# Normalized tiles scaled by two engines, Fourier sums taken token tile by token tile, and the last product by column halves

## The chip, the cores and the metric

The kernel runs on one NeuronCore of one Trainium2 chip. The metric is the device time of one execution in microseconds; a number for a kernel is the median of several runs. One execution was also taken by the hardware profiler, and all times of single instructions come from that one.

## The reference, cut to what matters

The program is two transformer blocks over 256 tokens of width 1024, in float32. The first block has two mixers (a gated linear recurrence and a spatial gate), a gated feed-forward part and a gated embedding; the second has a Fourier mixer, a retention mixer and two feed-forward parts. What the change touches:

```
h = rmsnorm(x, g) * (1 + scale) + shift        # at each boundary; the first block has no scale and shift
f = fftn(h.reshape(B, S, 4, 256), axes=(1, 3), norm="ortho").real     # Fourier mixer
x = x + gate * (f.reshape(B, S, D) @ w_fourier_out)
x = x + gate * swiglu(modulate(rmsnorm(x)))    # feed-forward, the last product is "down2"
return modulate(rmsnorm(x, final_norm_g), shift_final, scale_final)
```

The real part of the Fourier transform is a sum of products with cosine and sine tables: first over the 256 features of a group, then over the 256 tokens.

## The kernel before

**Weights.** All weights come through one stream of 238 chunks of 1 MB (128 x 2048 float32), issued by SP in a fixed order into three `raw` buffers; a buffer is free when `raw_done` says that its chunk was split. A chunk is split in two parts for TensorE: ScalarE copies it rounded (`w_hi`, L743), VectorE subtracts (`w_lo`, L1097). `tick(w)` does this for chunk `w + 4`, on ScalarE and on VectorE, and it stands at fixed places in each engine's program; four chunks of `w_hi` and `w_lo` are kept. The order of work on each engine is written out by hand, and an engine never takes a later instruction first.

**Products.** Each product is three matmuls (low by high, high by high, high by low). There are two token tiles of 128. `outer` (L477) takes the two tiles of a product into one of two PSUM `pair` buffers each, with the last four chunks first for tile 0 and then for tile 1. `wide_part` (L416) takes one chunk for one token tile: twelve matmuls of 512 columns, over half of the 1024 features.

**Boundaries.** At a boundary (`norm0` to `norm6`) the residual of a tile is updated (L1187, L1189, or L1177, L1180 in the first block), ScalarE squares it (L765), VectorE makes the mean (L1124), GpSimd the power (L355), VectorE scales it to `xn` (L1134). TensorE turns `xn` to features by partitions: eight transposes (L495), in two jobs of four, each in one of three `tp` banks. In `scaled` (L1145) VectorE then multiplies each of the eight 128 x 128 quarters with a column constant, and adds one where there is a shift, and leaves them in `hb` (or in `outb` at the end). For each half ScalarE rounds `hb` to `ht_hi` (L761) and VectorE subtracts to `ht_lo` (L1157), as `norm_his` and `norm_jobs`. `turned_head` starts the next product and waits for both halves of a tile before its first matmul. A quarter is one instruction; a half has four.

**Fourier mixer.** For tile 0, TensorE multiplies the four feature groups with the tables (L654, job `dft1`), then makes the gate rows (L517, job `rows0`), then turns tile 1, then the features of tile 1 (`dft1b`). The results are split to `tt_hi` and `tt_lo`. Only then come the token sums (L668, job `dft2`), for both tiles together in `tp` banks, which are split to `ht_hi` and `ht_lo` for the product `fo`. The modulation of tile 0 (`norm2`) is turned behind chunk 1 of the second tile of product `pleg`.

**The end.** After the last product `down2`, the second tile's residual, square, mean, power, `xn`, turn and eight quarters follow one another, each over the full width; four output transfers (L341) go out by SP.

Semaphores touched: `norm_read` and `fin_read` count halves read by VectorE; `lo_done` counts all splits; `w_used` the chunks used; `half_ready` tile 0 of a product.

## Time and profile before

| | us |
|---|---|
| median of 3 runs | 1191.15 (1190.08 to 1191.34) |
| profiled execution, own time | 1189.39 |
| span of that execution | 1187.2 |
| TensorE busy | 1146.8 |
| VectorE busy | 851.0 |
| ScalarE busy | 521.0 |
| a weight chunk, issue to landing | 4.9 |

The span runs from the first to the last instruction; the execution's own time is 2.2 us longer. A row of a timeline says when an instruction started, how long it took, its engine, line, what it wrote and read, how many were merged in it, and in brackets how long the engine had been idle and what ended that.

### The profile page before, as it was taken

The page shows a single profiled execution, that of the slowest core. Times are in us where ns is not written, and L with a number is a line of the kernel's source. Part 1 is how long each engine was busy: PE and PEld are TensorE (multiplying, and loading weights), DVE is VectorE, ACT ScalarE, POOL GpSimd, SP SyncE. Part 2 cuts the span into 40 slices and gives each one's busy share as a digit, 9 for nine tenths or more (in the row PEclk, how much of TensorE's full clock was granted, in tenths as well). Part 3 has the DMA queues.
Part 4 walks back from the last instruction along what each step waited for, and adds up shares of the span by engine and source line. Part 5 has one row for each costly group of instructions (what it writes and reads, how often), then busy time and mean ns, then how long its engine had stood idle before and what let it go on. Part 6 is the DMA issues. An engine that isn't in the chain of part 4 may idle for free.

```text
span 1187.2 us, 13991 instructions
## 1 busy us (share of the span) xinstructions
PE 1146.8 (97%) x5824; PEld 965.3 (81%) x5824; DVE 851.0 (72%) x1009; ACT 521.0 (44%) x463; POOL 27.4 (2%) x51
## 2 busy tenths in 40 slices
PE   6999999999899999998999999999999999999996
PEld 5898998888688888877778888879976887888885
DVE  5789988986667677575657767478955867767755
ACT  5556555634444344444343434334423433434430
POOL 1000000000000000000000000000001000000000
PEclk8999999999999999999999999999999999999998
DMA  8754563547357768532357777448753563786761
GB/s 310 280 213 163 187 231 130 176 167 269 142 205 258 301 265 316 204 141 72 138 181 272 262 305 290 191 177 320 278 202 122 212 249 142 255 311 259 287 234 36
DMA packets 38638, 259.81 MB, mean 219 GB/s; under 512 B 4144, under 2 KB 6448, under 8 KB 7856
## 3 DMA queue, kind: packets, MB, share of 16 engines
q1 hardware_dynamic: 36960, 251.84, 57.0%
q0 software_dynamic: 1616, 7.08, 1.6%
q8 instruction: 46, 0.75, 0.2%
q14 instruction: 16, 0.13, 0.0%
HBM read 257.86 MB, written 1.05 MB: 218 GB/s over the span
## 4 chain that ended last, share of the span: by engine, by line
PE 85%; DVE 9%; issue 3%; ACT 2%; DMA 1%; POOL 0%; SPq 0%; DVEq 0%; POOLq 0%; ACTq 0%
PE pair L416 41%; PE pair L477 24%; PE pair L442 10%; DVE w_lo L1097 4%; PE tp L495 2%; PE tp L554 2%; DVE hb L1145 2%; PE tp L716 1%; PE tp L668 1%; DMA raw<-stream 1%; ACT w_hi L743 1%; PE tp L581 1%; ACT ht_hi L761 1%; PE tp L694 1%; DVE ht_lo L1157 1%
## 5 line engine op out<-in xcount | busy, mean ns | idle before, releaser
L1097 DVE TENSOR_TENSOR w_lo<-raw,w_hi 128x2048 fp32r<-128x2048 f32 x182 | 412.8, 2288 | 92.8 <-ACT w_hi L743 92.6
L743 ACT ACTIVATE w_hi<-raw 128x2048 fp32r<-128x2048 f32 x182 | 347.6, 1916 | 223.9 <-DMA raw<-stream 133.3
L416 PE MATMUL pair<-w_hi,ht_lo 128*128 128x512 f32 x816 | 327.9, 402 | 20.8 <-DVE w_lo L1097 12.2
L416 PE MATMUL pair<-w_lo,ht_hi 128*128 128x512 f32 x816 | 319.8, 392 | 0.0
L416 PE MATMUL pair<-w_hi,ht_hi 128*128 128x512 f32 x816 | 319.7, 392 | 0.0
L416 PEld LDWEIGHTS pair<-w_hi,ht_lo 128*128 128x128 f32 x816 | 154.3, 189 | 57.6 <-issue 14.7
L416 PEld LDWEIGHTS pair<-w_lo,ht_hi 128*128 128x128 f32 x816 | 154.2, 189 | 33.1
L416 PEld LDWEIGHTS pair<-w_hi,ht_hi 128*128 128x128 f32 x816 | 154.5, 189 | 31.3 <-issue 1.2
L477 PE MATMUL pair<-w_hi,gt_lo 128*128 128x512 f32 x360 | 142.3, 395 | 0.2 <-DVE gt_lo L1163 0.2
L477 PE MATMUL pair<-w_lo,gt_hi 128*128 128x512 f32 x360 | 140.3, 390 | 0.0
L477 PE MATMUL pair<-w_hi,gt_hi 128*128 128x512 f32 x360 | 140.1, 389 | 0.0
L1106 DVE SCALAR_TENSOR_TENSOR raw<-raw,crow 128x1024 f32<-128x1024 f32 x112 | 132.4, 1220 | 1.3 <-DMA raw<-stream 1.3
L1218 DVE TENSOR_TENSOR prod<-prod,pair 128x512 f32<-128x512 f32 x33 | 22.7, 689 | 111.2 <-ACT prod L842 111.2
L842 ACT ACTIVATE prod<-pair 128x512 f32<-128x512 f32 x33 | 19.7, 598 | 179.1 <-PE pair L416 179.1
L442 PE MATMUL pair<-ht_hi,w_lo 128*128 128x256 f32 x320 | 91.0, 284 | 0.0
L442 PE MATMUL pair<-ht_lo,w_hi 128*128 128x256 f32 x320 | 90.6, 283 | 0.0
L442 PE MATMUL pair<-ht_hi,w_hi 128*128 128x256 f32 x320 | 90.6, 283 | 0.0
L477 PEld LDWEIGHTS pair<-w_hi,gt_lo 128*128 128x128 f32 x360 | 67.6, 188 | 14.6 <-DVE gt_lo L1163 0.7
L477 PEld LDWEIGHTS pair<-w_lo,gt_hi 128*128 128x128 f32 x360 | 67.6, 188 | 14.3
L477 PEld LDWEIGHTS pair<-w_hi,gt_hi 128*128 128x128 f32 x360 | 67.7, 188 | 14.1 <-issue 0.5
L442 PEld LDWEIGHTS pair<-ht_hi,w_hi 128*128 128x128 f32 x320 | 61.4, 192 | 0.1
L442 PEld LDWEIGHTS pair<-ht_hi,w_lo 128*128 128x128 f32 x320 | 61.4, 192 | 0.1
(201 smaller groups left out, 1101.8 us busy)
## 6 DMA issues: line engine op xcount, KB each, us to landing
raw<-stream SPq DMA_DIRECT2D x238, 1024.0 KB, 4.9
xres<-x SPq DMA_DIRECT2D x2, 512.0 KB, 6.8
prow<-rows POOLq DMA_DIRECT2D x1, 1024.0 KB, 9.7
xres<-x POOLq DMA_DIRECT2D x2, 512.0 KB, 4.9
dt<-decay POOLq DMA_DIRECT2D x1, 1024.0 KB, 7.1
outT<-outb SPq DMA_DIRECT2D x4, 256.0 KB, 2.2
csr<-dft POOLq DMA_DIRECT2D x1, 768.0 KB, 4.4
crow<-rows POOLq DMA_DIRECT2D x1, 512.0 KB, 6.4
```

What stands on the lines that cost most here:

```text
L416: mm = pe.matmul(pair[use % 2][:, t, :], a[:, 4 * c + k, t * P:(t + 1) * P], b[:, w % WS, k * 512:(k + 1) * 512], start=(c == 0 and k == 0 ...
L442: mm = pe.matmul(pair[use % 2][:, c, m * S:(m + 1) * S], a[:, k, m * P:(m + 1) * P], b[:, k, :], start=(k == 0 and n == 0), stop=(k == KT ...
L477: mm = pe.matmul(pair[(use + t) % 2][:, half, :], src(a, k0 + 2 * c + k, t), wsp[b][:, (w + c) % WS, k * D + half * 512:k * D + half * 512 ...
L495: mm = pe.transpose(tp[k % BANKS][:, n * P:(n + 1) * P], a, idn[:])
L554: mm = pe.matmul(tp[k % BANKS][:, hd * P:(hd + 1) * P], sk[:, hd, s * P:(s + 1) * P], sq[:, hd, s * P:(s + 1) * P], start=True, stop=True)
L581: mm = pe.matmul(tp[k % BANKS][:, hd * P:(hd + 1) * P], at[:, s, hd, t * P:(t + 1) * P], vv[:, s, (HH * half + hd) * P:(HH * half + hd + 1 ...
L743: sc.activation(w_hi[:, w % WS, :], raw[:, n % RAW, :], ACT.Copy).then_inc(hi_done, 1)
L842: sc.activation(prod[:, j % 2, :, :], pair[(use + j) % 2][:, :, 0:256], ACT.Silu).then_inc(silu_done, 1)
L1097: v.tensor_tensor(w_lo[:, w % WS, :], raw[:, n % RAW, :], whi32[:, w % WS, :], ALU.subtract).then_inc(raw_done, 1)
L1106: ins = v.scalar_tensor_tensor(out=src, in0=src, scalar=1.0, in1=crow[:], op0=ALU.mult, op1=ALU.mult, accum_out=mod[:, 2 * a + half:2 * a ...
L1145: ins = v.tensor_scalar(dst(k, half)[:, m * P:(m + 1) * P], tp[k % BANKS][:, m * P:(m + 1) * P], scale[:, f:f + 1], None if shift is None ...
L1218: v.tensor_tensor(prod[:, j % 2, :, :], prod[:, j % 2, :, :], pair[(use + j) % 2][:, :, 256:512], ALU.mult).then_inc(evac[(use + j) % 2], 1)
```

## The change

- Each tile's second half of quarters goes to ScalarE: `norm_scaled` scales (and shifts) four quarters with `Identity` activations, between the two `ht_hi` of the tile. VectorE's `scaled` keeps the first half. Two semaphores `norm_act` and `fin_act` count ScalarE's halves.
- `turned_head` waits for each half of a tile's features by itself, in front of the chunk that needs it.
- `norm_jobs` can put a `tick` between the two `ht_lo` (`between`), at norm1, norm3, norm4 and norm5. At norm1 other ticks move as well, on both engines.
- Fourier mixer: the turn of `norm2` tile 0 stands half a chunk later; token sums are taken for one token tile at a time, and accumulate in the two `pair` buffers that the product `fo` uses; the gate rows come after them; the ticks move.
- Boundary constants (`columns`) are made ahead of the residual.
- `down2` takes tile 1's last four chunks by column halves (`outer_by_halves`); the last residual, square and `xn` go by halves; eight matmuls on `ones` stand before the last turn.

The diff, cut to its core:

```diff
@@ PSUM jobs
-             ("rows0", 2, "row_copied"), ("norm2b", 2, "norm"), ("dft1b", 4, "split"), ("dft2", 4, "split"),
+             ("norm2b", 2, "norm"), ("rows0", 2, "row_copied"), ("dft1b", 4, "split"),
@@ turned_head
-                wait_split(split, 2)
                 for c in range(4):
                     wait_chunk(w + c)
+                    if c < 2:
+                        wait_split(split, c + 1)
...
-                wait_split(split, 4)
                 for c in range(4):
+                    if c < 2:
+                        wait_split(split, 3 + c)
@@ new: outer_by_halves, behind the last t == 0 chunk
+                for c in range(n - 4, n):
+                    mm = part(c, 1, 0)
+                mm.then_inc(last_half, 1)
+                for c in range(n - 4, n):
+                    part(c, 1, 1).then_inc(w_used, 1)
+                    if c == n - 3:
+                        tail()
@@ pleg and Fourier, TensorE
-                         (1, 1): turn_tile("norm2", xn, 0, xn_done, 5)})
+                  between={(2, 1): turn_tile("norm2", xn, 0, xn_done, 5)},
...
+            features("dft1", 0)
+            wait_evac(pe, USE["pleg"])
+            wait_evac(pe, USE["pleg"] + 1)
+            tokens("dft1", 0, (0, 1))
+            turn_tile("norm2", xn, 1, xn_done, 6)()
+            tokens("dft1", 0, (2, 3))
+            gate_rows("rows0", 1)
+            wait_split("norm2b", 2)
+            features("dft1b", 1)
+            tokens("dft1b", 1, range(4))
             outer(W0["fo"], 4, USE["fo"], tiles(ht),
-                  before={(c, 0): lambda c=c: wait_split("dft2", c + 1) for c in range(4)},
+                  before={(c, 0): lambda c=c: pe.wait_ge(mix_lo, max(c + 1, 2)) for c in range(4)},
@@ last turn, TensorE
-            turn_tile("norm6", xn, 1, xn_done, 14)()
+            for _ in range(8):
+                pe.matmul(warm[:, 384:512], ones[:], ones[:], start=True, stop=True)
+            for half in range(2):
+                pe.wait_ge(xn_done if half else xn_half, {0: 1, 1: 14}[half])
+                turn(tile_job("norm6", 1) + half, [xn[:, 1, (4 * half + k) * P:(4 * half + k + 1) * P] for k in range(4)])
@@ ScalarE
+            def norm_scaled(name, t, scale, shift, dst):
+                k = tile_job(name, t) + 1
+                act.wait_ge(tp_done, k + 1)
+                if k in SPLIT:
+                    at_least(act, lo_done, SPLIT[k] - 1)
+                for m in range(4):
+                    f = 4 + m
+                    ins = sc.activation(dst[:, m * P:(m + 1) * P], tp[k % BANKS][:, m * P:(m + 1) * P], ACT.Identity,
+                                        scale=scale[:, f:f + 1], bias=0.0 if shift is None else shift[:, f:f + 1])
+                ins.then_inc(sem(RELEASE[k][0]), 1)
+            def norm_his(name, t, scale, shift=None):
+                norm_hi(name, t, 0)
+                norm_scaled(name, t, scale, shift, hb[:, (tile_job(name, t) + 1) % 2, :])
+                norm_hi(name, t, 1)
@@ ScalarE, Fourier, after norm_his("norm2", t)
+            gate_rows("rows0", grow[0])
+            dft_his("dft1b", 1, (0, 1, 2))
+            tick(w - 2)
+            dft_his("dft1b", 1, (3,))
...
+            mix_his((0, 1))
+            tick(w - 1)
+            mix_his((2, 3))
+            tick(w)
@@ VectorE
+            def norm_jobs(name, t, scale, shift=None, between=None):
+                k = tile_job(name, t)
+                scaled(name, t, scale, shift, hb[:, k % 2, :])
+                dve.wait_ge(norm_read, RELEASE[k][1])
+                norm_lo(name, t, 0)
+                if between is not None:
+                    tick(between)
+                norm_lo(name, t, 1)
@@ VectorE, norm1
-                norm(RQ["mix"] + 2 * t + 1, t, w + 2 if t else None)
+                norm(RQ["mix"] + 2 * t + 1, t, w + 2 if t else w)
                 if t:
                     tick(w + 3)
-                norm_jobs("norm1", t, colv("ffn_pre", 0, 8))
-                if t == 0:
-                    tick(w)
-                    tick(w + 1)
+                norm_jobs("norm1", t, colv("ffn_pre", 0, 8), between=None if t else w + 1)
@@ VectorE, Fourier
                 norm_jobs("norm2", t, moda[:, 0, :], mod[:, 0:8])
-                if t == 0:
-                    tick(w - 3)
+            tick(w - 3)
+            dft_los("dft1b", 1, (0, 1, 2))
+            tick(w - 2)
+            dft_los("dft1b", 1, (3,))
@@ VectorE, boundary
+                if columns is not None:
+                    columns()
                 gated_post(0, use, w, halves, row, rows)
                 norm(q, 0)
-                if columns is not None:
-                    columns()
-                norm_jobs(name, 0, scale, shift)
-                tick(w - 3)
+                norm_jobs(name, 0, scale, shift, between=w - 3)
                 tick(w - 2)
@@ VectorE, last tile, for half in range(2)
+                dve.wait_ge(w_used, W0["down2"] + GROUPS) if half else dve.wait_ge(last_half, 1)
+                part = slice(half * 512, (half + 1) * 512)
+                link(v.tensor_tensor(xn[:, 1, part], pair[use % 2][:, half, :], grow[1][:, part], ALU.mult))
+                v.tensor_tensor(xres[:, 1, part], xres[:, 1, part], xn[:, 1, part], ALU.add).then_inc(x_ready, 1)
+                dve.wait_ge(ss_done, SS[q] + half)
```

## Rows read from the trace of the kernel before

**Rows 1.** The head of the page: span; busy time and instructions of each engine.

```profile
span 1187.2 us, 13991 instructions
PE 1146.8 (97%) x5824; PEld 965.3 (81%) x5824; DVE 851.0 (72%) x1009; ACT 521.0 (44%) x463; POOL 27.4 (2%) x51
```

**Rows 2.** Waits of TensorE: total us, times, longest.

```profile
PE pair L416 <- DVE w_lo L1097: 12.2, 5, 7.2
```

**Rows 3.** The chain that ended last: start, duration, instructions merged.

```profile
542.40 5.78 PE tp L654 x24
548.18 11.51 PE tp L668 x96
...
620.61 10.92 PE pair L416 x48
```

**Rows 4.** Timeline of TensorE at norm4.

```profile
775.32 0.47 PE L416 MATMUL pair<-w_hi,ht_lo 128*128 128x512 f32 x1 [0.53 <-issue]
...
782.07 0.50 PE L416 MATMUL pair<-w_hi,ht_lo 128*128 128x512 f32 x1 [1.02 <-DVE w_lo L1097]
...
789.77 0.50 PE L416 MATMUL pair<-w_hi,ht_lo 128*128 128x512 f32 x1 [1.02 <-DVE ht_lo L1157]
```

**Rows 5.** Timeline of VectorE at norm4.

```profile
768.91 2.64 DVE L1145 TENSOR_SCALAR hb<-tp,moda,mod 128x128 f32<-128x128 f32 x8 [0.75 <-PE tp L495]
...
772.93 4.49 DVE L1097 TENSOR_TENSOR w_lo<-raw,w_hi 128x2048 fp32r<-128x2048 f32 x2
777.33 1.22 DVE L1187 TENSOR_TENSOR xn<-pair,grow 128x1024 f32<-128x1024 f32 x1
```

**Rows 6.** Groups of ScalarE by form: busy us, mean ns, idle before.

```profile
L761 ACT ACTIVATE ht_hi<-hb 128x512 fp32r<-128x512 f32 x24 | 15.0, 630 | 35.4 <-DVE hb L1145 35.2
...
L752 ACT ACTIVATE vr<-pair 128x1024 f32<-128x1024 f32 x4 | 4.1, 1020 | 11.1 <-PE pair L416 11.1
...
L752 ACT ACT_TABLE_LOAD x2 | 2.6, 1283 | 0.0
```

**Rows 7.** Timeline of ScalarE and VectorE at the start, norm0 tile 0.

```profile
12.08 1.13 ACT L761 ACTIVATE ht_hi<-hb 128x512 fp32r<-128x512 f32 x2
...
14.00 4.49 DVE L1097 TENSOR_TENSOR w_lo<-raw,w_hi 128x2048 fp32r<-128x2048 f32 x2
```

**Rows 8.** Timeline of VectorE and TensorE at norm1.

```profile
304.46 4.49 DVE L1097 TENSOR_TENSOR w_lo<-raw,w_hi 128x2048 fp32r<-128x2048 f32 x2
...
306.84 0.47 PE L416 MATMUL pair<-w_hi,ht_lo 128*128 128x512 f32 x1 [2.79 <-issue]
...
314.47 0.50 PE L416 MATMUL pair<-w_hi,ht_lo 128*128 128x512 f32 x1 [1.91 <-DVE w_lo L1097]
...
323.23 0.50 PE L416 MATMUL pair<-w_hi,ht_lo 128*128 128x512 f32 x1 [0.53 <-DVE ht_lo L1157]
```

**Rows 9.** Sums over a stretch at norm1, with the granted clock (PEclk).

```profile
315.00:319.00 4.00, 4.00 (x12) 3.06 (x11) 2.95 (x2) 0.20 (x1) 0.11 (x1) 0.57 0.73 262
```

**Rows 10.** Timeline of TensorE from the turn of norm2 to tile 1's features.

```profile
522.07 0.66 PE L495 MATMUL tp<-idn,xn 128*128 128x128 f32 x4 [1.01 <-DVE xn L1134]
...
536.64 1.12 PE L517 MATMUL tp<-dg,ones 128*128 128x512 f32 x2 [1.59 <-DVE tt_lo L1163]
...
542.40 0.50 PE L654 MATMUL tp<-cs_hi,ht_lo 128*128 128x512 f32 x1 [3.76 <-DVE ht_lo L1157]
```

**Rows 11.** Timeline of VectorE and TensorE behind the last product.

```profile
1175.44 1.23 DVE L1187 TENSOR_TENSOR xn<-pair,grow 128x1024 f32<-128x1024 f32 x1 [0.48 <-PE pair L477]
...
1180.76 1.97 PE L495 MATMUL tp<-idn,xn 128*128 128x128 f32 x8 [5.36 <-DVE xn L1134]
...
1181.92 2.64 DVE L1145 TENSOR_SCALAR outb<-tp,moda,mod 128x128 f32<-128x128 f32 x8 [1.21 <-PE tp L495]
```

**Rows 12.** Transfers on the page: KB each, median us from issue to landing.

```profile
raw<-stream SPq DMA_DIRECT2D x238, 1024.0 KB, 4.9
```

More of the change, by code:

```diff
@@ L135, in plan_psum @@
                 splits += 1
-            sem = {"norm": "norm_read", "split": "lo_done"}.get(kind, kind)
+            half = (k - jobs[name]) % 2
+            sem = {"norm": ("norm_read", "norm_act")[half], "fin_read": ("fin_read", "fin_act")[half],
+                   "split": "lo_done"}.get(kind, kind)
             if kind == "split":
@@ L455, in turned_head, with outer @@
                         norm()
-                wait_split(split, 4)
                 for c in range(4):
+                    if c < 2:
+                        wait_split(split, 3 + c)
                     wide_part(w + c, use + c // 2, c % 2, 1)
-            def outer(w, n, use, src, k0=0, before={}, after={}):
+            def outer(w, n, use, src, k0=0, before={}, between={}, after={}):
                 m = max(0, n - 4)
@@ L474, in outer @@
                     for half in range(2):
+                        if half and (c, t) in between:
+                            between[c, t]()
                         for k in range(2):
@@ L642, in _, with features @@
                   before={(0, 0): lambda: wait_split("tx", 2), (0, 1): lambda: wait_split("tx", 4)},
-                  after={(1, 0): turn_tile("tx", xres, 1, x_ready, 4),
-                         (1, 1): turn_tile("norm2", xn, 0, xn_done, 5)})
+                  between={(2, 1): turn_tile("norm2", xn, 0, xn_done, 5)},
+                  after={(1, 0): turn_tile("tx", xres, 1, x_ready, 4)})
             wait_split("norm2", 2)
             pe.wait_ge(cs_done, 1)
-            for t in range(TT):
+            def features(name, t):
                 for gr in range(4):
-                    k = JOB["dft1b" if t else "dft1"] + gr
+                    k = JOB[name] + gr
                     claim(k)
@@ L905, in head_gates, with boundary @@
                 tick(W0[b] + 1)
-            def boundary(w, q, name, n_x):
+            def boundary(w, q, name, n_x, scale, shift):
                 norm_squares(q, 0, n_x)
@@ L912, in boundary @@
                 tick(w - 2)
-                norm_his(name, 0)
+                norm_his(name, 0, scale, shift)
                 tick(w - 1)
@@ L916, in boundary @@
                 tick(w)
-                norm_his(name, 1)
+                norm_his(name, 1, scale, shift)
             def gated_chunks(half, name0, plan):
@@ L1062, in _ @@
                 tick(w)
-            boundary(W0["ro"] + 7, RQ["norm5"], "norm5", 11)
+            boundary(W0["ro"] + 7, RQ["norm5"], "norm5", 11, moda[:, 3, :], mod[:, 72:80])
             ffn("ffn2", "h2")
@@ L1070, in _ @@
                     hidden_his("h2", GROUPS - 1)
-            for t in range(TT):
-                norm_squares(RQ["norm6"] + t, t, 13 + t)
+            norm_squares(RQ["norm6"], 0, 13)
+            norm_scaled("norm6", 0, moda[:, 4, :], mod[:, 96:104], outb[:, 1, :])
+            for half in range(2):
+                act.wait_ge(x_ready, 14 + half)
+                part = slice(half * 512, (half + 1) * 512)
+                sc.activation(xn[:, 1, part], xres[:, 1, part], ACT.Square,
+                              accum_out=st[:, RQ["norm6"] + 1, 0, half:half + 1]).then_inc(ss_done, 1)
+            norm_scaled("norm6", 1, moda[:, 4, :], mod[:, 96:104], outb[:, 3, :])
         @block.vector
@@ L1150, in norm_jobs @@
-            def norm_jobs(name, t, scale, shift=None):
-                scaled(name, t, scale, shift, lambda k, half: hb[:, k % 2, :])
-                for half in range(2):
-                    k = tile_job(name, t) + half
-                    dve.wait_ge(norm_read, RELEASE[k][1])
-                    dve.wait_ge(t_hi, SPLIT[k] + 1)
-                    where = (slice(None), slice(4 * half, 4 * half + 4), slice(t * P, (t + 1) * P))
-                    v.tensor_tensor(ht[1][where], hb[:, k % 2, :].rearrange("p (k s) -> p k s", k=4), ht32[where],
-                                    ALU.subtract).then_inc(lo_done, 1)
+                k = tile_job(name, t)
@@ new lines, in scaled @@
+                dve.wait_ge(tp_done, k + 1)
+                if k in SPLIT:
+                    at_least(dve, lo_done, SPLIT[k] - 1)
+                for f in range(4):
+                    ins = v.tensor_scalar(dst[:, f * P:(f + 1) * P], tp[k % BANKS][:, f * P:(f + 1) * P],
+                                          scale[:, f:f + 1], None if shift is None else shift[:, f:f + 1],
+                                          ALU.mult, *(() if shift is None else (ALU.add,)))
+                ins.then_inc(sem(RELEASE[k][0]), 1)
```

188 lines of the change are left out of this document (114 added, 74 removed).

## The prediction

> **What bounds the kernel now.** I read the page first. TensorE is busy 1146.8 us of a 1187.2 us span, VectorE 851.0 [rows 1], so an edit pays only where it shortens TensorE's queue of work or takes out one of its waits. About 40 us are waits, and the list of waits puts the largest entry, 12.2 us in five places, on VectorE's weight splits `w_lo` [rows 2]. The timeline shows where: none inside the long products, all at the normalization boundaries, at the Fourier stage, at the start and at the end. So I walked these places in the timelines of the three engines.
>
> Two paces carry the rest. Forty-eight matmuls of 512 columns take 10.92 us, 0.227 us each, so one weight chunk for one token tile (12 of them) is 2.73 us [rows 3]. An idle time in a row counts from a modelled end 0.17 us after the next possible start, so a stall is its idle time plus 0.17.
>
> **The boundaries of norm3, norm4 and norm5** look alike; I use norm4. TensorE stalls three times there, idle 0.53, 1.02 and 1.02 us [rows 4], or 0.70, 1.19 and 1.19 by start times. VectorE's order is the cause: eight `hb` quarters (2.64 us), two `ht_lo`, then both `w_lo` (4.49 us) from 772.93, then the second tile's residual at 777.33 [rows 5]. The first stall waits for the first `w_lo`, the second for the third, the last for tile 1's `ht_lo`.
>
> The change gives four quarters to ScalarE, lets the product start after half the features, and puts `tick(w-3)` between the two `ht_lo`. VectorE's four quarters take 1.32, from 768.91 to 770.27. ScalarE's `ht_hi` (0.63 [rows 6]) ends at 770.94, `ht_lo` needs 0.61 net of overlap, and the first `w_lo` ends at 773.87, before TensorE's 774.63. Stall one is gone. The second `ht_lo` and `w_lo` end by 776.6, so the residual starts 0.74 earlier than 777.33. All that follows up to the third `w_lo` is one chain on VectorE and keeps that 0.74: TensorE goes on at 781.33, not 782.07, having waited 1.25. TensorE arrives 0.69 earlier and stall two stays about as long as it was. On tile 1 the first `ht_lo` comes at 787.65; TensorE needs it at 787.84. Stall three (1.19) goes, with a margin of 0.2 only. Its second half has one chunk, 2.73 us, more. Gain 1.93 for a boundary; norm5 gets 0.05 more because its constants move from behind `xn` into an idle wait. Three boundaries: **5.85** (4.5 if the 0.2 is missed by half a microsecond each time, 6).
>
> **ScalarE's four quarters** have no row. The 128x1024 form takes 1.02 and the 128x512 `hb` form 0.63 [rows 6]; two forms of 512 back to back overlap by 0.1 (1.13 for two at the start [rows 7]). Taken down to 128 columns this gives 0.27 for one and 0.81 for four; as slow as four full 512-column ones it is 2.1. What two pointer operands cost on ScalarE no row shows. I take the middle, 1.45. VectorE's constants cost time too (four with two constants 1.32), so I don't go to the low end.
>
> The Trainium skill, page "ScalarE: Activation LUTs", section "What ACT_TABLE_LOAD costs", says that each per-partition pointer operand adds 93 ns, which speaks against moving scale and shift here: by it four take 1.64 us with both and 1.27 with a scale alone, and the sum below would fall by about 0.6 us.
>
> **norm1** has other stalls: TensorE idle 2.79 and 1.91, then 0.53 [rows 8]. `tick(w)` moves ahead of the mean square: that `w_lo` (2.2) fills an idle 1.2 and delays `xn` of tile 0 to 300.82, so the turn waits 0.6 us, a new stall. But the next product's first chunk is then split, and its `ht_lo` is there at 304.0: TensorE starts it at 304.5, not 306.84. VectorE then has one `w_lo` and four quarters fewer before the mean square, which comes at 306.72 rather than 308.86. ScalarE's second square pass needs `hi` of half 1 first and ends at 306.3, in time. The chain behind it keeps the 2.14, so TensorE resumes at 312.33 after a 2.40 stall. With stall three gone (0.69) that is 2.83. In the profile the clock stood at 0.57 of full speed in 315 to 319 us, right behind the idle 1.91 [rows 9]; twelve matmuls took 4.45 instead of 2.9, a loss of 1.5. The new stall is longer but single; whether the clock falls there I can't tell. I count a quarter of it: **3.2** (2.8 to 4.3).
>
> **norm0** loses. VectorE's first `w_lo` waits behind both `ht_lo` (from 14.00 [rows 7]), and the second now waits for ScalarE's `ht_hi` (end 12.71 for the first), four quarters and another `ht_hi`: `w_lo` begins at about 15.4 and TensorE at 17.7 instead of 16.43, 1.27 later. TensorE runs there at half speed until 21.7, so the late start costs between half of this and all; the stall before tile 1 (0.70) goes. Net **-0.4** (-1.2 to +0.2).
>
> **Fourier stage.** Removed: a stall before the turn of tile 0 (idle 1.01), one before the gate rows (1.59) and one before tile 1's features (3.76) [rows 10]. The turn now sits half a chunk later, at 522.26, behind `xn`'s end at 522.02. The last product ends at 527.2 rather than 528.4; tile 0's second `ht_lo` goes over ScalarE (524.96 + 1.45 + 0.63 + 0.69, with handovers 527.7), so 0.55 is waited. Then TensorE has 24 feature matmuls (5.46), half the token sums of tile 0 (2.9), a turn (0.85), the other half (2.9), the gate rows (1.75), features (5.46) and token sums (5.76). A group of 24 took 5.78 and all 96 token matmuls 11.51 [rows 3]; their number is unchanged, only their order, and they accumulate in the two `pair` banks. That adds to 25.1, end 552.85, against 559.53. Covers: the `xn` of tile 1 is ready at 534.65, the turn comes at 536.1. Its second `ht_lo` comes at 541.5, the token sums and gate rows cover it to 541.6. The last `tt_lo` is behind `tick(w-2)` and comes at 551.5, 0.15 late. `tick(w-3)` moves from 527.9 to 541.4, past `dft1`, the norm and their queues: VectorE frees its raw slot at 543.7 only, so SP, which waits for `raw_done` in stream order, issues the next chunk fourteen microseconds later. With 4.9 us to land [rows 12] it is there by 549, split by 558.3 and wanted at 560.8. `gate_rows` on ScalarE goes behind the norm, and features 1 and 2 of tile 1 now claim its banks; the copies end by 542, wanted at 543 and 544.4. The new wait on `mix_lo` needs two `ht_lo` by 552.45, before the sums end. **6.5** (5.3 with 2.1 for the quarters, 7.1 with 0.81).
>
> **The end.** TensorE's order in the last product changes, not its work: columns 0 to 511 of tile 1 are ready at 1169.1, the rest at 1175.44 as before. But VectorE's four quarters of tile 0 stand ahead in its queue until 1173.63. Then half 0: two ops of 0.69 and ScalarE's square reach 1175.7, VectorE waiting for `ss_done` with half 1's product queued behind it; half 1 so starts at 1175.95, and not at 1175.44, and its square is read at 1178.12; before it was 1179.11. `xn` comes in halves of 0.45, so the first turn starts at 1179.47 against 1180.76 [rows 11]. Eight matmuls on ones keep TensorE busy to about 1177. Before, eight transposes took 1.97 there, against 1.09 elsewhere. Warm, ScalarE ends its quarters at 1181.95, cold at 1182.9; before, VectorE ended at 1184.56, and 2.64 us of output DMA follow in both cases. Gain 2.6 or 1.7: **2.2** (1.0 to 2.9).
>
> **Sum.** -0.4 + 3.2 + 6.5 + 5.85 + 2.2 = 17.35 us. The span becomes 1169.85, the profiled execution's own time 1189.39 - 17.35 = 1172.0. The median of the runs shown is 1.76 above that execution, so I forecast 1191.15 - 17.35 = **1173.8 us**. The low and high ends of the terms give 12.4 and 20.5, 1178.8 and 1170.7.
>
> **Rivals.**
> - The sums of the Fourier stage don't cover: lo parts in ScalarE's and VectorE's strict order come late once more, as 3.76 shows they do today. With half of that stage's 6.5 lost: 1177.1. Chance 0.15.
> - The quarters take 2.1: start -0.65, Fourier -1.2, end -0.65, boundaries nothing: 1176.3. Chance 0.12.
> - Slower: ScalarE loads a table around the scaled copies. A load takes 1.28 [rows 6]. Up to 2.2 us for the four, the boundaries hide them; beyond it each microsecond costs about 12 (two tiles at six places). The gain left at 2.2, 14.4 us, is gone at 3.4 us. Two loads around each group make 4.0: 7 us slower, 1198. Against it: `Copy` and `Square` run among Silu, Gelu, Exp and Sigmoid everywhere here, and ScalarE has eleven loads in 463 instructions [rows 1, 6], none ahead of a `Copy`; a scaled copy is of that kind. Chance 0.05, of which 0.04 slower and 0.01 about even.
> - The clock stays up at norm1 and the plain runs lose more to it than the profiled one: 1171.3. Chance 0.06.
>
> For the table load, the same page of the Trainium skill, "Table sets: the hidden batching unit", says that identity and copy are in every set, so no load would come; that agrees with the rows of `Copy`.
>
> The forecast itself keeps 0.62, with 1172 to 1176 of its own. The range that leaves out two in ten at most is **1170.5 to 1179.5**. Same means within 0.2%, 2.4 us, about what this measurement can tell: faster 0.94, same 0.02, slower 0.04.
>
> **What the new profile should show.** No stall before the first chunk of `rva`, one of about 1.25 before its third, none before tile 1. Identity activations of 128x128 in groups near 1.45. At norm1 one stall of 2.4 and a turn 0.6 late. At the Fourier stage at most 0.7 us of idle TensorE and `fo` starting some 6.5 us earlier. At the start, TensorE 1.3 later. Wrong would be: groups above 2.2 us, table loads among them, the third-chunk stall growing beyond 2, or `fo` waiting for `mix_lo`.

## The result, and the profile after

The changed kernel takes 1172.26 us (median of 4 runs, 1171.27 to 1173.09); before, on the same chip, 1190.62. The ratio is 0.9846, with a 95% interval of 0.9829 to 0.9863: 1.5% faster. The forecast was 1173.8 in 1170.5 to 1179.5. The profiled execution takes 1173.02 with a span of 1170.1, 17.1 us shorter than [rows 1]; the sum had said 17.35.

The head of the page after: span, busy times, instructions.

```profile
span 1170.1 us, 14019 instructions
PE 1145.0 (98%) x5840; PEld 966.8 (83%) x5840; DVE 835.0 (71%) x957; ACT 539.3 (46%) x521; POOL 27.5 (2%) x51
```

TensorE works as long as before (1145.0 against 1146.8): the gain is waits. To see where it arises, follow one matmul through both traces, by its start. A stage's gain is the step in the last column.

| matmul of the products | before | after | after minus before |
|---|---|---|---|
| first of all | 16.43 | 17.60 | +1.17 |
| `zi`, third chunk | 95.80 | 97.52 | +1.73 |
| `ffn0`, tile 1, second chunk | 328.80 | 326.27 | -2.53 |
| first of `fo` | 559.53 | 550.54 | -8.99 |
| `ffn1`, tile 1, second chunk | 603.20 | 592.21 | -10.98 |
| `rva`, tile 1, second chunk | 795.38 | 782.44 | -12.94 |
| `ffn2`, tile 1, second chunk | 1004.03 | 989.15 | -14.87 |
| last of `down2` | 1175.01 | 1160.14 | -14.87 |
| end | 1187.2 | 1170.1 | -17.1 |

**A boundary.** TensorE at norm4 after, the rows that answer to [rows 4]:

```profile
763.65 0.39 PE L428 MATMUL pair<-w_hi,ht_lo 128*128 128x512 f32 x1
...
770.41 0.50 PE L428 MATMUL pair<-w_hi,ht_lo 128*128 128x512 f32 x1 [1.16 <-DVE w_lo L1196]
```

Three stalls have become one: the first chunk has no bracket, the third waits 1.16 + 0.17, tile 1 (at 776.96) doesn't wait. VectorE's queue there, answering to [rows 5]:

```profile
757.93 1.36 DVE L1242 TENSOR_SCALAR hb<-tp,moda,mod 128x128 f32<-128x128 f32 x4 [0.75 <-PE tp L550]
760.06 0.69 DVE L1252 TENSOR_TENSOR ht_lo<-hb,ht_hi 128x512 fp32r<-128x512 f32 x1 [0.77 <-ACT ht_hi L834]
760.67 2.28 DVE L1196 TENSOR_TENSOR w_lo<-raw,w_hi 128x2048 fp32r<-128x2048 f32 x1
762.87 0.69 DVE L1252 TENSOR_TENSOR ht_lo<-hb,ht_hi 128x512 fp32r<-128x512 f32 x1
```

Read the brackets: the first `ht_lo` waits for ScalarE, the second doesn't, because the `w_lo` between them lasts longer than ScalarE's chain. That chain, from ScalarE's timeline:

```profile
759.33 0.63 ACT L834 ACTIVATE ht_hi<-hb 128x512 fp32r<-128x512 f32 x1
759.86 1.49 ACT L848 ACTIVATE hb<-tp,mod,moda 128x128 f32<-128x128 f32 x4
761.38 0.63 ACT L834 ACTIVATE ht_hi<-hb 128x512 fp32r<-128x512 f32 x1
```

Four quarters take 1.49 (1.45 assumed). By form (busy us, mean ns):

```profile
L848 ACT ACTIVATE hb<-tp,mod,moda 128x128 f32<-128x128 f32 x32 | 11.9, 452 | 0.0
L848 ACT ACTIVATE hb<-tp,col 128x128 f32<-128x128 f32 x16 | 4.5, 363 | 0.0
```

**Fourier stage.** TensorE's waits after, for [rows 10]; the turns and the gate rows stand without a bracket:

```profile
519.75 1.04 PE L550 MATMUL tp<-idn,xn 128*128 128x128 f32 x8
525.26 0.50 PE L713 MATMUL tp<-cs_hi,ht_lo 128*128 128x512 f32 x1 [0.35 <-DVE ht_lo L1252]
533.71 1.03 PE L550 MATMUL tp<-idn,xn 128*128 128x128 f32 x8
537.45 1.88 PE L572 MATMUL tp<-dg,ones 128*128 128x512 f32 x4
```

**norm1** for [rows 8]: one stall is left in the product, beside the small new one ahead of the turn.

```profile
302.64 1.09 PE L550 MATMUL tp<-idn,xn 128*128 128x128 f32 x8 [0.45 <-DVE xn L1233]
314.26 0.50 PE L428 MATMUL pair<-w_hi,ht_lo 128*128 128x512 f32 x1 [2.27 <-DVE w_lo L1196]
```

**The end** for [rows 11]: ones, a wait, and a turn of 1.09, not 1.97.

```profile
1160.37 1.95 PE L798 MATMUL warm<-ones 128*128 128x128 f32 x16
1164.61 1.09 PE L550 MATMUL tp<-idn,xn 128*128 128x128 f32 x8 [2.30 <-DVE xn L1748]
```

### The profile page after: what moved, and what is told of

It is laid out like the page before. It is cut to its first block, busy times and chain, and to the rows that moved or that the text cites. A ratio compares the mean times of both kernels' runs of the same rounds, so it can differ in the third digit from the quotient of the medians.

```text
span 1170.1 us, 14019 instructions
## 1 busy us (share of the span) xinstructions
PE 1145.0 (98%) x5840; PEld 966.8 (83%) x5840; DVE 835.0 (71%) x957; ACT 539.3 (46%) x521; POOL 27.5 (2%) x51
## 4 chain that ended last, share of the span: by engine, by line
PE 83%; DVE 9%; DMA 3%; issue 2%; ACT 2%; POOL 1%; SPq 0%; POOLq 0%; ACTq 0%; DVEq 0%
PE pair L428 42%; PE pair L493 20%; PE pair L454 7%; PE pair L509 4%; DVE w_lo L1196 4%; PE tp L550 3%; PE tp L612 2%; DMA raw<-stream 2%; DMA mskf<-masks 1%; PE tp L785 1%; PE pair L724 1%; PE tp L713 1%; ACT w_hi L816 1%; PE tp L639 1%; PE tp L763 1%
## 5 line engine op out<-in xcount | busy, mean ns | idle before, releaser
L493 PE MATMUL pair<-w_hi,gt_lo 128*128 128x512 f32 x272 | 107.3, 395 | 0.3 <-DVE gt_lo L1268 0.3
L493 PE MATMUL pair<-w_lo,gt_hi 128*128 128x512 f32 x272 | 106.0, 390 | 0.0
L493 PE MATMUL pair<-w_hi,gt_hi 128*128 128x512 f32 x272 | 105.9, 389 | 0.0
L454 PEld LDWEIGHTS pair<-ht_lo,w_hi 128*128 128x128 f32 x320 | 61.4, 192 | 0.0
L493 PEld LDWEIGHTS pair<-w_hi,gt_lo 128*128 128x128 f32 x272 | 51.1, 188 | 11.2 <-DVE gt_lo L1268 0.7
L493 PEld LDWEIGHTS pair<-w_lo,gt_hi 128*128 128x128 f32 x272 | 51.1, 188 | 10.7
```

Of the source, the lines that this page charges most:

```text
L454: mm = pe.matmul(pair[use % 2][:, c, m * S:(m + 1) * S], a[:, k, m * P:(m + 1) * P], b[:, k, :], start=(k == 0 and n == 0), stop=(k == KT ...
L493: mm = pe.matmul(pair[(use + t) % 2][:, half, :], src(a, k0 + 2 * c + k, t), wsp[b][:, (w + c) % WS, k * D + half * 512:k * D + half * 512 ...
```

## The experiments

The profile agrees with the sum as a whole; two terms in it don't (start, norm1). The runs built on the changed kernel are called its siblings. Four experiments ask what each part is worth, four undo or slow one device each, and four look at the clock and put a better version together. The kernel before, run beside each of these three groups, had medians of 1190.22, 1190.53 and 1190.09 us. In the diffs `norm_all` stands for VectorE's eight quarters followed by the two `ht_lo`, and `fill(n)` for n matmuls on ones into `warm`.

### Norm0 without sharing

```diff
-            norm_his("norm0", 0, colv("mix_pre", 0, 8))
+            norm_hi("norm0", 0, 0)
+            norm_hi("norm0", 0, 1)
...
-            norm_jobs("norm0", 0, colv("mix_pre", 0, 8))
+            norm_all("norm0", 0, colv("mix_pre", 0, 8))
```

> The changed kernel with one part undone: all eight quarters of norm0, of both tiles, on VectorE again, in the order quarters, quarters, ht_lo, ht_lo; ScalarE takes both ht_hi one behind the other. My theory: the lateness of 1.7 us that the changed kernel carries from its start to the products of norm1 begins with VectorE's first w_lo, 1.26 us later than before (15.26 against 14.00), and all of VectorE's and the raw ring's work up to 97 us hangs on it. So the first product starts at 16.4 us again and not at 17.6, the first w_lo at 14.0, and by 97 us TensorE is 1.7 us earlier than in the changed kernel: span 1168.4 instead of 1170.1, median near 1170.6. The rival: only the first 1.2 us hang on it, and the other half microsecond is a transfer (mask or raw slot) that lands when it lands: 0.5 to 0.7 us less in the end, since the stall of 0.7 before tile 1 comes back. A third: the start is hidden by stalls of later stages and the span stays at 1170.

Measured: 1171.72 us, ratio 0.985 (0.9833 to 0.9866), span 1169.9. VectorE's first `w_lo` starts at 14.26 (14.00 before, 15.26 in the changed kernel), and TensorE at

```profile
16.60 0.79 PE L428 MATMUL pair<-w_hi,ht_lo 128*128 128x512 f32 x1 [7.36 <-DVE w_lo L1198]
```

So far my theory. But the span hardly moved: TensorE left norm1's stall 1.70 earlier (312.56 against 314.26), and began tile 1 only 0.20 earlier (320.63 against 320.83). The windows there (stretch, its length, TensorE's busy time and count, granted clock, DMA share, GB/s) show why. First this run, then the changed kernel:

```profile
312.00:316.00 4.00, 3.44 (x8) 0.57 0.60 205
316.00:320.00 4.00, 4.00 (x23) 1.00 0.79 293
```

```profile
312.00:316.00 4.00, 1.74 (x8) 1.00 0.24 55
316.00:320.00 4.00, 4.00 (x23) 1.00 0.78 285
```

Behind the same stall (2.45 here, 2.43 there) the clock was at its lower level, 1.2 GHz, in one profile and stayed at 2.4 GHz in the other. From the stall to tile 1 it took 8.07 here and 6.57 there: 1.50 lost. The edit touches nothing there, and the clock fell at this place in some siblings and not in others (below, "norm1"), so I don't put it down to the edit. Nor is all of the 1.7 at the start the edit's (below, "the start").

### The end as before

```diff
-            down("down2", "h2", after={(4, 1): lambda: gate_rows("rows3", 4)},
-                 tail=turn_tile("norm6", xn, 0, xn_done, 13))
-            for _ in range(8):
-                pe.matmul(warm[:, 384:512], ones[:], ones[:], start=True, stop=True)
+            down("down2", "h2", after={(4, 1): lambda: gate_rows("rows3", 4),
+                                       (GROUPS - 2, 1): turn_tile("norm6", xn, 0, xn_done, 13)})
+            turn_tile("norm6", xn, 1, xn_done, 14)()
```

ScalarE's last square and VectorE's last residual and `xn` go over the full width again as well.

> The changed kernel with the end of before: the last product in the order of the other down products, the final norm of tile 1 in one piece of 1024 columns, no matmuls on ones ahead of the last turn; ScalarE keeps its four quarters of each tile of norm6. My theory: the halves and the clock make nearly all of the 2.2 us of the end. The last product ends at 1160.4, the turn starts 5.5 us behind it at 1165.9 (as 1175.24 to 1180.76 before), its eight transposes take 1.97 at half clock, ScalarE's quarters end at 1169.4 and the span is 1172.2, 2.1 longer. The rival: the sharing of the quarters made most of it (2.64 us of VectorE's become 1.3), and the halves only fill VectorE's queue: then the span grows by 0.5 us at most.

Measured: 1173.7 us, ratio 0.9861 (0.9844 to 0.9878), span 1172.2.

```profile
1166.06 1.97 PE L550 MATMUL tp<-idn,xn 128*128 128x128 f32 x8 [5.36 <-DVE xn L1225]
```

The wait of 5.36 and the slow turn are those of [rows 11]. From the last product matmul to the end: 12.19 before, 11.89 here, 9.96 in the changed kernel. Halves and ones make 1.93 of the end's 2.23, sharing 0.30.

### Norm1 to norm5 without sharing, new order kept

```diff
-                norm_jobs(name, 0, scale, shift, between=w - 3)
+                norm_all(name, 0, scale, shift, between=w - 3)
```

and so for tile 1, norm1 and norm2.

> The changed kernel with the quarters of norm1, norm2, norm3, norm4 and norm5 all on VectorE (eight for each tile), while the new orders stay: tick between the two ht_lo, the product's waits by half of the features, norm0 and norm6 shared. My theory: sharing and order each make a part. The first stall of a boundary stays away (ht_lo of half 0 and the first w_lo still come before TensorE). The second grows from about 1.3 to 1.9 us, since VectorE's work ahead of the second residual is again that of before, and the third comes back with 0.5 to 1.1. So some 1.5 us for each of norm3, norm4 and norm5, as much at norm1, a few tenths at norm2: span 4 to 7.5 us longer, about 1176, median near 1178. The rival: the order (waits by halves, tick in between) makes the gain alone and ScalarE's half only moves idle time: span at most 1 us longer.

Measured: 1174.92 us, ratio 0.9871 (0.9853 to 0.9889), span 1170.5. The start of this execution was early by 1.29, so the span hides the loss; by steps: the three boundaries lose 0.82, 0.79 and 0.82, norm1 0.10, and the Fourier stage gains 0.79. Net 1.7. My 4 to 7.5 was far too much and the rival's 1 nearer: the new order keeps 3.45 of the boundaries' 5.88 by itself, and sharing adds 2.43. The second stall grows, the third stays at 0.3:

```profile
769.66 0.50 PE L428 MATMUL pair<-w_hi,ht_lo 128*128 128x512 f32 x1 [1.54 <-DVE w_lo L1197]
```

At the Fourier stage sharing even costs. VectorE alone, tile 0:

```profile
519.20 1.37 DVE L1243 TENSOR_SCALAR hb<-tp,moda,mod 128x128 f32<-128x128 f32 x4 [0.89 <-PE tp L550]
520.48 1.36 DVE L1265 TENSOR_SCALAR hb<-tp,moda,mod 128x128 f32<-128x128 f32 x4
521.76 0.68 DVE L1253 TENSOR_TENSOR ht_lo<-hb,ht_hi 128x512 fp32r<-128x512 f32 x1
522.61 0.69 DVE L1253 TENSOR_TENSOR ht_lo<-hb,ht_hi 128x512 fp32r<-128x512 f32 x1 [0.17 <-ACT ht_hi L834]
```

and shared, in the changed kernel:

```profile
520.39 1.37 DVE L1242 TENSOR_SCALAR hb<-tp,moda,mod 128x128 f32<-128x128 f32 x4 [0.89 <-PE tp L550]
522.52 0.69 DVE L1252 TENSOR_TENSOR ht_lo<-hb,ht_hi 128x512 fp32r<-128x512 f32 x1 [0.77 <-ACT ht_hi L834]
524.52 0.69 DVE L1252 TENSOR_TENSOR ht_lo<-hb,ht_hi 128x512 fp32r<-128x512 f32 x1 [1.30 <-ACT ht_hi L834]
```

The second `ht_lo` starts 3.41 behind the first quarter in the one, 4.13 in the other. ScalarE does `ht_hi`, quarters, `ht_hi` one behind the other, and here no `w_lo` fills VectorE's wait.

### Before, with norm1's stalls filled

```diff
+                if split == "norm1":
+                    fill(8)
                 wait_split(split, 2)
                 for c in range(4):
+                    if c == 2 and split == "norm1":
+                        fill(6)
                     wait_chunk(w + c)
```

> The kernel before, with matmuls on ones put into its two stalls at norm1: 8 ahead of the wait for the first half product of ffn0, 6 ahead of its third chunk; nothing else is changed, and both groups end before what they precede is ready. My theory: the changed kernel gained 4.28 us at norm1 and not 3.2, because its TensorE clock doesn't fall there; before, it stood at 0.57 in 315 to 319 us behind the second stall, and that cost 1.5 us. With the stalls filled the clock stays up and the span of before falls by 1.3 to 1.6 us, from 1187.2 to about 1185.7. The rival: the clock falls there whatever TensorE does, or the queue's chain makes up for it: span unchanged within 0.3 us. In that case the changed kernel's extra microsecond at norm1 is queue and not clock.

Measured: 1189.54 us (12 runs), ratio 0.9995 (0.9984 to 1.0006), span 1188.2: neither theory. At norm1 the clock stayed up and TensorE was 1.77 earlier at tile 1 (321.46 against 323.23), 0.25 of which it had at 95 us already; that leaves 1.5, as I had said. At the Fourier stage all of it went again and more:

```profile
540.00:544.00 4.00, 3.38 (x8) 0.50 0.00 0
544.00:548.00 4.00, 4.00 (x13) 0.64 0.00 0
```

There, behind the stall of 3.76 [rows 10], the clock now stood at half; in the first profile it had been at 1.00. From the restart behind that stall to the first product of `fo` it takes 20.01 here and 17.13 in the first profile, with no other wait between them: a loss of 2.9 us (the 2.6 in later expectations was my low reading).

### Waits for whole tiles

```diff
+                wait_split(split, 2)
                 for c in range(4):
                     wait_chunk(w + c)
-                    if c < 2:
-                        wait_split(split, c + 1)
...
+                wait_split(split, 4)
                 for c in range(4):
-                    if c < 2:
-                        wait_split(split, 3 + c)
```

> The changed kernel with one wait put back: ahead of the products behind norm0, norm1, norm3, norm4 and norm5, TensorE waits for both ht_lo of a tile and not for the half of the features that its chunk reads. My theory: tile 0 loses nothing at norm3 to norm5 (the second ht_lo ends at 763.56, the product starts at 763.65), tile 1 loses the third stall's whole length: its second ht_lo ends at 778.77 where TensorE is ready at 776.96, since it now stands behind ScalarE's quarters and its second ht_hi. 1.8 us for each of the three, 5.4, as much or less at norm1, and about 1 at the start: span 1176 to 1178. The rival: the two halves come so close together that waiting for both costs what it did before, 1.19: 3.6 in all, span 1173.7; or nothing.

Measured: 1181.69 us, ratio 0.992 (0.9905 to 0.9936), span 1179.4. The third stall at norm4 and, alike, at norm3 and norm5:

```profile
784.18 0.50 PE L428 MATMUL pair<-w_hi,ht_lo 128*128 128x512 f32 x1 [1.72 <-DVE ht_lo L1250]
```

With what follows each, the boundaries are 1.97, 1.94 and 2.01 us longer, as worked out (1.8); tile 0 loses nothing. Norm1, with the lower clock in this execution, lost 2.8. So the half waits aren't a trimming: without them the sharing would make each third stall longer than before.

### No `w_lo` between the two `ht_lo`

```diff
-                norm_jobs(name, 0, scale, shift, between=w - 3)
+                norm_jobs(name, 0, scale, shift)
+                tick(w - 3)
```

> The changed kernel with tick(w-3) behind both ht_lo at norm3, norm4 and norm5 and not between them. My theory: VectorE then waits for ScalarE's quarters and second ht_hi with nothing in hand (ht_hi ends at 762.01) and starts the first w_lo at 762.7 and not at 760.67; that ends at 764.9, where TensorE is ready at 763.65: a first stall of 1.3 us, and the second residual comes 1.4 later, so that the second stall stays as it is. 1.4 us for each of the three boundaries, span 1174.3. The rival: the stall only moves, the second one shrinks by what the first grows: span within 0.5 of 1170.1.

Measured: 1177.48 us, ratio 0.988 (0.9865 to 0.9895), span 1173.2 with a start 1.0 earlier.

```profile
765.43 0.50 PE L428 MATMUL pair<-w_hi,ht_lo 128*128 128x512 f32 x1 [1.19 <-DVE w_lo L1196]
...
772.23 0.50 PE L428 MATMUL pair<-w_hi,ht_lo 128*128 128x512 f32 x1 [1.06 <-DVE w_lo L1196]
```

The first stall is back with 1.36, and the second is only 0.1 shorter. The boundaries are 1.39, 1.34 and 1.39 us longer, the 1.4 of my theory.

### Token sums last

```diff
-            tokens("dft1", 0, (0, 1))
             turn_tile("norm2", xn, 1, xn_done, 6)()
-            tokens("dft1", 0, (2, 3))
             gate_rows("rows0", 1)
             wait_split("norm2b", 2)
             features("dft1b", 1)
+            tokens("dft1", 0, range(4))
             tokens("dft1b", 1, range(4))
```

> The changed kernel with TensorE's order at the Fourier stage as before: turn of tile 1 and gate rows right behind tile 0's features, then tile 1's features, and all token sums, of both tiles, behind them; sums still go into the pair banks and VectorE's and ScalarE's orders stay. My theory: the gain of 6.5 us there is the cover that tile 0's token sums give. Without it TensorE waits 2.5 us for xn of tile 1 (ready at 533.3, features end at 530.8) and 2.8 more for its second ht_lo: 5.3 us, span 1175.4. The rival: the gain is from VectorE's and ScalarE's shorter queues (no w_lo and four quarters fewer ahead of the norm): then at most 1.5 us are lost. By what the first four runs showed of the clock, a stall of over 2.4 us can cost up to 2.6 us of half clock behind it; so up to 1178.

Measured: 1180.34 us, ratio 0.9902 (0.988 to 0.9924), span 1178.3.

```profile
534.35 1.07 PE L550 MATMUL tp<-idn,xn 128*128 128x128 f32 x8 [1.51 <-DVE xn L1232]
...
540.06 0.50 PE L713 MATMUL tp<-cs_hi,ht_lo 128*128 128x512 f32 x1 [2.32 <-DVE ht_lo L1251]
```

Two stalls, 1.68 and 2.49 with the 0.17 for each, make 4.2 where I had 5.3, and the clock fell behind the second (0.60 in 540 to 544 us). From there to the first product of `fo` it takes 18.74; the same matmuls take 17.09 in the run with both places filled (below), where the clock was at 1.00. So of the stage's 6.4 more, 4.2 are waits, 1.65 the clock, and 0.6 is not traced (the gate rows take 2.31, not 1.88). The kernel before had no loss of clock here. Set against it, the cover makes about 4.8 of the stage's 6.46, my estimate from 6.43 less 1.65. The other 1.65 stayed although the sums stood last: it belongs to what this run left in place, the later turn and the shorter queues of the rival, and no run takes these apart.

### ScalarE's quarters slower

```diff
                 for m in range(4):
                     f = 4 + m
+                    sc.activation(junk[:, m, :], tp[k % BANKS][:, m * P:m * P + 28], ACT.Identity, scale=scale[:, f:f + 1],
+                                  bias=0.0 if shift is None else shift[:, f:f + 1])
                     ins = sc.activation(dst[:, m * P:(m + 1) * P], tp[k % BANKS][:, m * P:(m + 1) * P], ACT.Identity,
```

> The changed kernel with ScalarE's four quarters made slower: ahead of each of them one more activation of the same kind on 28 columns, into a buffer that nobody reads. A group of four should take some 1.1 us more, 2.6 instead of 1.49. This asks for the price of a microsecond of ScalarE in that place, which the prediction put at nothing for the boundaries up to 2.2 us, at 3.85 us per microsecond for start, Fourier stage and end together, and at about 12 beyond 2.2: by that 4.2 + 0.4 x 8 = 7.5 us, span 1177.6. My theory now: the half waits still cover most of it at the boundaries (0.25 by VectorE's chain and 0.2 by the second ht_lo of tile 1, 1.4 us for three), Fourier 2.1, end 1.1, start 0.5: 5.1 us, span 1175.2.

Measured: 1178.8 us, ratio 0.9888 (0.987 to 0.9906), span 1176.7. A group takes 2.57, 1.08 more. The first two of a group in ScalarE's timeline:

```profile
764.35 0.36 ACT L849 ACTIVATE junk<-tp,mod,moda 128x28 f32<-128x28 f32 x1
764.61 0.45 ACT L851 ACTIVATE hb<-tp,mod,moda 128x128 f32<-128x128 f32 x1
```

The Fourier stage pays 2.08, the boundaries 0.61, 0.56 and 0.57, the end 0.98: 4.8 us. The span's 6.6 holds another 1.5 at norm1, where the clock fell in this execution, and 0.3 at the start. My 5.1 for the parts holds, 4.8 and the 0.3. The recorded prices would have given 7.5: 4.2 for start, Fourier stage and end, which measure 3.4 (the start costs less than its price), and 3.2 for the boundaries and norm1 beyond 2.2, which measure 1.7 at the three boundaries and nothing at norm1 besides the clock. At norm4 the second stall grows by 0.26 (idle 1.42, not 1.16), and tile 1's second chunk, which doesn't wait in the changed kernel, starts 0.2 late behind `ht_lo`. One point doesn't tell at which length of the group the boundaries begin to pay.

### Before, with both places filled

As the run with norm1 filled, and in addition:

```diff
                     turn_tile("norm2", xn, 1, xn_done, 6)()
+                    fill(14)
                     wait_split("norm2b", 2)
```

> The kernel before, with matmuls on ones in its stalls at norm1 (8 and 6, as in the run with these alone) and 14 more ahead of the wait for the second ht_lo of norm2's tile 1, in the stall of 3.9 us. My theory, formed on the first runs: behind every stall of 2 to 4 us the clock falls in some executions and not in others. The kernel before has two such places (norm1: 1.5 us lost in its profile, nothing at the Fourier stage; with norm1 filled the profile lost 2.6 us at the Fourier stage). With both filled neither loses: span 1187.2 - 1.8 = 1185.4, median about 1187, 3 us below before, and the executions lie closer together (before 1187.25 to 1193.81). The rival: the clock falls somewhere else instead, as it did when norm1 alone was filled: span 1187 to 1188.5, median within 1 us of before.

Measured: 1187.91 us (11 runs), ratio 0.9984 (0.9975 to 0.9992), span 1185.7.

```profile
312.00:316.00 4.00, 3.40 (x21) 1.00 0.51 170
316.00:320.00 4.00, 4.00 (x23) 1.00 0.85 281
540.00:544.00 4.00, 3.37 (x17) 1.00 0.01 4
544.00:548.00 4.00, 4.00 (x25) 1.00 0.00 0
```

Full clock at both places, 2.2 us off the median (3 expected), and the executions lie in 3.3 us (1186.58 to 1189.86) where those of before, taken beside them, spread over 6.0 (1186.75 to 1192.76).

### The changed kernel, norm1 filled

```diff
                 for c in range(4):
+                    if c == 2 and split == "norm1":
+                        for _ in range(8):
+                            pe.matmul(warm[:, 384:512], ones[:], ones[:], start=True, stop=True)
                     wait_chunk(w + c)
```

> The changed kernel with 8 matmuls on ones ahead of norm1's third chunk, in the stall of 2.4 us. My theory: behind that stall the clock fell in five of eight profiles of the changed kernel and its variants and cost 1.3 to 1.7 us each time. Filled, it never falls there: granted clock 1.00 in 312 to 320, k-th products of ffn0 as in the changed kernel's profile, and the median 0.8 us lower than 1172.26. The rival: the clock falls at the next place with a wait (Fourier stage, boundaries), and the median stays.

Measured: 1171.25 us, ratio 0.9845 (0.9832 to 0.9859), span 1168.5; the clock is 1.00 in 312 to 320 us. The median is 1.0 lower, but the ratio is that of the changed kernel: by these runs the worth of the filling stays open.

### Without the ones at the end

```diff
-            for _ in range(8):
-                pe.matmul(warm[:, 384:512], ones[:], ones[:], start=True, stop=True)
```

> The changed kernel without the eight matmuls on ones ahead of the last turn. My theory: TensorE is idle from 1160.4 to 1164.6 and the clock is at its half by then: the turn's eight transposes take 1.97 instead of 1.09, ScalarE's quarters start 0.85 later, span 0.85 longer than with them. The rival: the wait of 2.3 us behind the ones is long enough for the clock to fall anyway (it stood at full until 1166.87), or ScalarE's and the transfer's times hide it: no difference.

Measured: 1174.03 us, ratio 0.9863 (0.985 to 0.9877), span 1171.6.

```profile
1165.45 1.97 PE L550 MATMUL tp<-idn,xn 128*128 128x128 f32 x8 [4.08 <-DVE xn L1746]
```

The turn takes 1.97, and from the last product to the end it is 10.62 against 9.96: the ones are worth 0.66 (0.85 expected), the halves 1.27.

### A kernel from the parts

Quarters on VectorE at norm0 and norm2, shared elsewhere, norm1 filled.

> A kernel put together from what the runs showed: the changed kernel, with all eight quarters on VectorE at norm0 (first product 0.7 earlier) and at norm2 (in the run with norm1 to norm5 on VectorE the Fourier stage was 0.8 shorter, since ScalarE's serial ht_hi, quarters, ht_hi gives the second ht_lo 0.7 later than VectorE alone does), shared at norm1 and norm3 to norm6, and norm1's stall filled. My theory: 0.3 from norm0 at 95 us, 0.8 from the Fourier stage, 0.8 on average from the clock: span 1168 to 1169 (that of the changed kernel is 1170.1, with 1.1 to 1.4 of chance lateness at its start), median near 1170.4. The rival: the terms don't add, as the start's difference is mostly chance: median within 0.5 of 1172.3.

Measured: 1169.27 us (5 runs, 1168.23 to 1170.43), ratio 0.9824 (0.9811 to 0.9838), span 1168.2. The Fourier stage is 0.75 shorter than the changed kernel's and has no wait left. This is the fastest of all; its interval and the changed kernel's still overlap a little.

## Why the prediction was right, and where it wasn't

**Boundaries** (5.85 recorded): 1.99, 1.96 and 1.93, together 5.88, step by step as worked out, the second stall at 1.32 (1.25). The margin of 0.2 for tile 1 held; the 0.05 more for norm5 doesn't show (1.93). What the prediction didn't weigh is how the gain divides: the half waits carry it (without them a boundary is 1.97 longer), the `w_lo` between carries 1.37, and sharing 0.81. These add up to more than the gain, since each covers for the others.

**ScalarE's quarters** (1.45 recorded): 1.49 with both constants, 1.12 with a scale alone. The Trainium skill, page "ScalarE: Activation LUTs", section "What ACT_TABLE_LOAD costs", gives 93 ns for each pointer operand; the rows give 452 - 363 = 89, so the step agrees, while the totals of a group estimated from that section's figures, 1.64 and 1.27, were each 0.15 too high here. By the prediction's own prices those totals would also have moved the sum by 0.4 (start +0.2, Fourier stage -0.35, end -0.2), not 0.6. The rival of table loads fell: there are eleven loads of 1.28 before and eleven after. That agrees with the same page of the Trainium skill, section "Table sets: the hidden batching unit", which has identity and copy in every set.

**Fourier stage** (6.5): 6.46, with the one wait foreseen (0.55 said, 0.52 measured); the 0.15 by which the last `tt_lo` was to be late doesn't show. The run with the sums last shows that their cover makes most of it, about 4.8; the rest is argued. I had not seen that VectorE alone would have been 0.8 better there.

**The end** (2.2): 2.23, of it halves 1.27, ones 0.66, sharing 0.30.

**The start** (-0.4): -1.73, the step that was mis-sized. The first product came 1.17 later (1.27 recorded) and the stall ahead of tile 1 went, as said (the first product moves by itself too: 16.91 to 17.95 in seven profiles with this start, 16.24 to 16.47 in three with that of before). But I let nothing happen from there to 97 us. TensorE's wait for the masked scores ends the start in every trace. The changed kernel's, and that of its sibling with norm1 filled, which has the same start:

```profile
96.61 1.16 PE L612 MATMUL tp<-sq,sk 128*128 128x128 f32 x8 [0.91 <-DVE at L1406]
```

```profile
94.96 1.16 PE L615 MATMUL tp<-sq,sk 128*128 128x128 f32 x8 [0.70 <-DVE at L1409]
```

Seven profiles with this start lie at 94.96 to 97.00 (median 95.58), the three with the start of before at 94.64 to 94.98 (median 94.88). By the medians the term is about -0.7, an estimate from few profiles, and the other microsecond is the spread of one execution. What I see of it comes in with the weight transfers. ScalarE's split that waits for one, in the same two traces:

```profile
48.42 1.91 ACT L816 ACTIVATE w_hi<-raw 128x2048 fp32r<-128x2048 f32 x1 [7.14 <-DMA raw<-stream]
```

```profile
46.97 1.92 ACT L819 ACTIVATE w_hi<-raw 128x2048 fp32r<-128x2048 f32 x1 [6.47 <-DMA raw<-stream]
```

VectorE's `w_lo` ahead of it was 0.51 apart (38.00 and 37.49), the landing 1.45. What moves a landing was not looked into. Nor is the first run's reading of 1.7 for norm0's sharing right: with quarters on VectorE the same wait ends at 94.96, and 95.16 in the last kernel, some 0.5 before the siblings' median.

**norm1** (+3.2): +4.26, the step that I could not tell. The queue part was 2.83 and is 2.8: the five siblings whose clock fell behind this stall, as it did before, gain 2.79 to 2.82 here. No run undid the move of norm1's ticks by itself, so its share is read from traces and not shown. The clock was counted with a quarter of 1.5, and in the profile it stayed up. That was luck of the execution: of eight profiles of the changed kernel and its siblings with this stall of 2.4 to 2.5 us, the clock fell behind it in five and stayed at 1.00 in three. In a ninth, with the waits for whole tiles, a stall of the same length stands ahead of the first chunk, and the clock fell behind it too. The two errors, -1.3 and +1.1, cancel; the sum's 17.35 against 17.1 looks better than its terms were.

**The median.** It moved by 18.4 us, more than the span did. The forecast put it 1.76 above the profiled execution, as before; it lies 0.76 below. That execution was forecast at 1172.0 and took 1173.02, since its own time is 2.9 longer than its span and not 2.2; why was not looked into. So 1.0 too little and 2.5 too much make the 1.5 between forecast and median, which is in part luck. The rival with a chance of 0.06 had the clock stay up at norm1, as the profile shows; that the plain runs of the kernel before lose more to the clock than its profiled one fits the medians, but no trace shows it.

## What to carry to other kernels

When work is handed to a second engine, look at what its serial chain (copy, share, copy) does to the last piece: at the Fourier stage, where no other job filled the first engine's wait, it came 0.7 us later and the stage was 0.8 longer than with one engine; at a boundary, with a job in that wait and a consumer that took halves, sharing was worth 0.8. When two profiles differ by a microsecond, follow one matmul through several executions before giving the microsecond to the change: here transfers and the clock each move that much by themselves. And a wait of 2 to 4 us cost more than its length in the executions where the clock fell behind it; matmuls on ones that ended before the wait did cost nothing there.

## What the runs showed of the hardware

- Behind one and the same wait the TensorE clock falls in one execution and not in the next. Behind norm1's stall (idle 2.3 us) it read 0.57 in 312 to 316 us in one profile and 1.00 in another; behind the 3.76 of the Fourier stage 0.50 in one and 1.00 in another, for a loss of 1.5 and of 2.9 us. Nor does the longer wait always cost it: in the profile of the kernel before the clock stayed at 1.00 behind norm1's first wait (idle 2.79, 307 to 312 us) and fell behind the next one (idle 1.91). Filled with ones, norm1 showed no fall in four profiles and the Fourier stage none in the one taken.
- An Identity activation of 128x128 out of PSUM takes 452 ns with scale and bias as columns and 363 with a scale alone; in a row of four each further one adds 0.35 and 0.25 us. One of 28 columns with both takes 379 on average of 40: the columns are the smaller part of it.
